# Nine feed-forward chunks instead of eleven carry modulation blocks, and the pooling stage eight instead of four

## The reference, cut to what matters

```
def trunk(x, c, ...):
    for i in range(2):
        shift1, scale1, gate1, shift2, scale2, gate2 = split(silu(c) @ w_ada[i] + b_ada[i], 6)
        h = rms_norm(x, g_mix[i]) * (1 + scale1) + shift1
        mix = attention(h) @ w_o            # layer 0: stick-breaking attention
        mix = pool_mixer(h, hist, w_pool)   # layer 1: trailing means over 2/4/8/16 frames, four 512x512 maps
        x = x + gate1 * mix
        h = rms_norm(x, g_ffn[i]) * (1 + scale2) + shift2
        x = x + gate2 * ((silu(h @ w_gate[i]) * (h @ w_up[i])) @ w_down[i])
```

## Time and profile before

| what | value |
|---|---|
| median of 3 runs | 3418.9 us (3418.2 to 3427.47) |
| the profiled execution | 3424.23 us |
| its span in the trace | 3422.4 us |
| TensorE busy | 3268.1 us, 95% of the span |
| VectorE busy | 2119.0 us, 62% |
| ScalarE busy | 1308.8 us, 38% |
| first feed-forward, about | 988 to 2182 us of the span |
| pooling stage with its norms, about | 2182 to 2317 us |
| second feed-forward, about | 2317 us to the end |

### The profile page before, as it was taken

How to read it: one execution, slowest core, us unless ns; L and a number is a source line. 1 busy time by engine, 2 the same in 40 slices (tenths; PEclk the granted TensorE clock), 3 DMA queues, 4 the chain that set the end, 5 groups by cost and what they waited for, 6 DMA issues and landing times.

```text
span 3422.4 us, 47948 instructions
## 1 busy us (share of the span) xinstructions
PE 3268.1 (95%) x20213; PEld 2952.9 (86%) x20213; DVE 2119.0 (62%) x1852; ACT 1308.8 (38%) x991; POOL 137.5 (4%) x124
## 2 busy tenths in 40 slices
PE   6999998889979999999999999769999999999999
PEld 3677776667979999999999999559999999999999
DVE  4488885557887767777776777784344443334443
ACT  3344444455453444344443443333322222332221
POOL 0000000000000000000000000100000000000000
PEclk9999999999989999999999999889999999999999
DMA  9777777877645555556555555544333333333341
GB/s 353 269 267 251 250 242 246 296 275 261 232 150 196 196 200 192 186 182 208 203 178 193 186 208 196 180 165 147 123 123 126 131 123 127 131 123 123 125 132 62
DMA packets 325816, 646.48 MB, mean 189 GB/s; under 512 B 10882, under 2 KB 13514, under 8 KB 325322
## 3 DMA queue, kind: packets, MB, share of 16 engines
q1 hardware_dynamic: 317144, 630.17, 54.1%
q10 hardware_dynamic: 8586, 15.09, 1.2%
HBM read 631.46 MB, written 14.74 MB: 189 GB/s over the span
## 4 chain that ended last, share of the span: by engine, by line
PE 87%; DVE 4%; DMA 4%; ACT 3%; issue 1%; ACTq 0%; POOL 0%; SPq 0%; DVEq 0%; POOLq 0%
PE bank L1495 24%; PE bank L1497 23%; PE bank L1496 23%; PE bank L1577 3%; PE bank L1522 3%; PE bank L1579 3%; PE bank L1578 3%; DMA raw<-in_w_ada 3%; PE bank L1683 1%; PE bank L1507 1%; DMA raw<-in_cache_k 1%; PE bank L1711 1%; PE bank L1712 1%; DVE w_lo L945 0%; PE bank L1531 0%
## 5 line engine op out<-in xcount | busy, mean ns | idle before, releaser
L945 DVE TENSOR_TENSOR w_lo<-raw,w_hi 128x2048 fp32r<-128x2048 f32 x323 | 738.9, 2290 | 877.7 <-ACT w_hi L568 877.7
L568 ACT ACTIVATE w_hi<-raw 128x2048 fp32r<-128x2048 f32 x323 | 616.3, 1915 | 1349.7 <-PE bank L1497 1169.4
L1495 PE MATMUL bank<-h_hi,w_hi 128*128 128x384 f32 x3136 | 1064.1, 339 | 33.0 <-DVE h_lo L1028 24.7
L1496 PE MATMUL bank<-h_lo,w_hi 128*128 128x384 f32 x3136 | 1052.1, 335 | 0.0
L1497 PE MATMUL bank<-h_hi,w_lo 128*128 128x384 f32 x3120 | 1047.8, 336 | 0.0
L1495 PEld LDWEIGHTS bank<-h_hi,w_hi 128*128 128x128 f32 x3136 | 591.8, 189 | 78.6 <-issue 69.1
L1496 PEld LDWEIGHTS bank<-h_lo,w_hi 128*128 128x128 f32 x3136 | 592.1, 189 | 0.0
L1497 PEld LDWEIGHTS bank<-h_hi,w_lo 128*128 128x128 f32 x3120 | 588.7, 189 | 0.0
L1495 PE MATMUL bank<-act_hi,w_hi 128*128 128x384 f32 x1408 | 473.1, 336 | 0.0
L1497 PE MATMUL bank<-act_hi,w_lo 128*128 128x384 f32 x1408 | 470.8, 334 | 0.0
L1496 PE MATMUL bank<-act_lo,w_hi 128*128 128x384 f32 x1408 | 470.7, 334 | 0.0
(11 more groups left out here) (225 smaller groups left out, 2506.1 us busy)
## 6 DMA issues: line engine op xcount, KB each, us to landing
raw<-in_w_ada SPq DMA_DIRECT2D x192, 1024.0 KB, 5.8
raw<-in_w_gate SPq DMA_DIRECT2D x88, 1024.0 KB, 5.2
raw<-in_w_up SPq DMA_DIRECT2D x88, 1024.0 KB, 5.2
raw<-in_w_down SPq DMA_DIRECT2D x88, 1024.0 KB, 5.1
raw<-in_w_qkv SPq DMA_DIRECT2D x40, 1024.0 KB, 5.3
raw<-in_cache_k SPq DMA_DIRECT2D x32, 1024.0 KB, 6.8
raw<-in_cache_v SPq DMA_DIRECT2D x32, 1024.0 KB, 7.7
raw<-in_w_o SPq DMA_DIRECT2D x15, 1024.0 KB, 5.1
```

Of the source, the lines that this page charges most:

```text
L568: act.activation(w_hi[:, s], raw[:, s], ACT.Copy).then_inc(hi_ready, 1)
L945: dve.tensor_tensor(w_lo[:, s], raw[:, s], w_hi[:, s].bitcast(f32), ALU.subtract).then_inc(lo_ready, 1)
L1495: pe.matmul(out, w, a, start=start, stop=False)
L1496: pe.matmul(out, w, al, start=False, stop=False)
```

## The change

The first feed-forward gets nine mixed chunks (`HOSTS`), eight in the loop and the ninth written out, and behind them two plain chunks, written out too, with the code of the second layer's chunks. So the last four blocks, the second layer's scale2, are no longer computed there. The pooling stage takes eight blocks: one before step 0, one at the end of each of the steps 0 to 6, behind the group's map where there is one. Every step has the transposes of a block. On ACT the copy to `mod` stands in every step, ahead of the two store DMAs instead of behind `h_hi`. SP loads eight blocks there, one after the other through the four slots, and the second feed-forward's first quarters behind them.

```diff
-W_POOL = W_FFN0 + 5 * CHUNKS
+HOSTS = 9
+W_PLAIN = W_FFN0 + 5 * HOSTS
+W_POOL = W_PLAIN + 3 * (CHUNKS - HOSTS)
-ADA_POOL = ADA_FFN + 2 * CHUNKS
+ADA_POOL = ADA_FFN + 2 * HOSTS
...
@@ SP
-            with sp.Fori(1, CHUNKS) as c:
+            with sp.Fori(1, HOSTS) as c:
                 load_mixed(W_FFN0 + c * 5, c, 1, c * 2 + (ADA_FFN - 24))
+            for c in range(HOSTS, CHUNKS):
+                W = W_PLAIN + 3 * (c - HOSTS)
+                load_cols(W, w_gate[0], c * 512)
+                load_cols(W + 1, w_up[0], c * 512)
+                load_down(W + 2, 0, c)
...
-            for i in range(3):
+            for i in range(7):
                 for s in range(4):
                     sp.wait_ge(ada_used, 4 * (ADA_QKV + i) + s + 1)
                     load_late(i + 1, s)
@@ ACT
-            def dense_chunk(W, c, last=False):
+            def dense_chunk(W, c, last=False, squares_after=False):
...
                 if not last:
-                    for n in range(12, 16):
-                        dense(W, n)
+                    for n in range(4):
+                        dense(W, 12 + n)
+                        if squares_after:
+                            square(2, n)
...
+                mod_out(4 * (ADA_QKV + j) + 4, ADA_POOL + j, 2, ada_used)
                 act.wait_ge(uT_taken, j + 1)
...
-                if j % 2 == 0:
-                    i = ADA_QKV + j // 2
-                    mod_out(4 * i + 4, ADA_POOL + j // 2, 2, ada_used)
@@ DVE
-            def dense_chunk(W, c, r, last=False):
+            def dense_chunk(W, c, r, last=False, sums_after=False):
...
                 for s in range(4):
-                    if not last:
+                    if not last and not (sums_after and s == 3):
                         dense(W, 12 + s)
-                    down_add(4 * W + 9 + s, s, r, 1)
+                    down_add(4 * W + 9 + s, s, r, 0 if isinstance(c, int) and c < CHUNKS else 1)
+                    if sums_after and s < 3:
+                        square_sum(2, s)
...
-            dense(W_FFN0 + 5 * (CHUNKS - 1), 23)
+            dense(W_POOL, 3)
...
-                if j % 2:
-                    mod_in(ADA_POOL + j // 2, 3, pieces=1)
+                mod_in(ADA_POOL + j, 3, pieces=1)
@@ PE
-            with pe.Fori(0, CHUNKS) as c:
+            with pe.Fori(0, HOSTS) as c:
                 mixed_chunk(W_FFN0 + c * 5, c, ADA_FFN + c * 2, R_FFN0 + c * 4, 4)
+            for c in range(HOSTS, CHUNKS):
+                dense_chunk(W_PLAIN + 3 * (c - HOSTS), c, R_FFN0 + c * 4, 4, half=1)
...
-                if j % 2:
-                    ada_turn(ADA_POOL + j // 2, 3)
-                elif j:
-                    ada_block(ADA_QKV + j // 2, 2)
+                ada_turn(ADA_POOL + j, 3)
                 if j >= 2 and j % 2 == 0:
                     map_group(j // 2 - 1)
+                if j < 7:
+                    ada_block(ADA_QKV + j + 1, 2)
```

More of the change, by code:

```diff
@@ L842, in gate_out, with mixed_chunk @@
                 act.activation(act_f[:], bank[:, 4:8, 0:TOK], ACT.Silu).then_inc(gate_taken, 1)
-            def mixed_chunk(W, c, a, following, last=False):
+            def mixed_chunk(W, c, a, following):
                 for n in range(4, 10):
@@ L858, in mixed_chunk @@
                     following(W, 20 + s)
-                    if last:
-                        square(2, s)
-            def dense_chunk(W, c, last=False):
+            def dense_chunk(W, c, last=False, squares_after=False):
                 for n in range(4, 7):
@@ L873, in dense_chunk @@
                 if not last:
-                    for n in range(12, 16):
-                        dense(W, n)
-            with act.Fori(0, CHUNKS - 1) as c:
+                    for n in range(4):
+                        dense(W, 12 + n)
+                        if squares_after:
+                            square(2, n)
+            with act.Fori(0, HOSTS - 1) as c:
                 mixed_chunk(W_FFN0 + c * 5, c, ADA_FFN + c * 2, mixed)
-            mixed_chunk(W_FFN0 + 5 * (CHUNKS - 1), CHUNKS - 1, ADA_FFN + 2 * (CHUNKS - 1), dense, last=True)
+            mixed_chunk(W_FFN0 + 5 * (HOSTS - 1), HOSTS - 1, ADA_FFN + 2 * (HOSTS - 1), dense)
+            for c in range(HOSTS, CHUNKS):
+                dense_chunk(W_PLAIN + 3 * (c - HOSTS), c, squares_after=c == CHUNKS - 1)
             root(2)
@@ L1368, in down_add, with mixed_chunk @@
                 add_quad(down_bank(s), 4 * s, layer, GATE2)
-            def mixed_chunk(W, c, a, layer, r, following, last=False):
+            def mixed_chunk(W, c, a, layer, r, following):
                 for n in range(4, 12):
@@ L1384, in mixed_chunk @@
                     down_add(4 * W + 17 + s, s, r, layer)
[L1385 to L1388, removed]
+                    following(W, 20 + s)
             def rows_out(q):
@@ L1402, in dense_chunk @@
                 for s in range(4):
-                    if not last:
+                    if not last and not (sums_after and s == 3):
                         dense(W, 12 + s)
-                    down_add(4 * W + 9 + s, s, r, 1)
+                    down_add(4 * W + 9 + s, s, r, 0 if isinstance(c, int) and c < CHUNKS else 1)
+                    if sums_after and s < 3:
+                        square_sum(2, s)
                     if last:
                         rows_out(s)
-            with loop(dve, 0, CHUNKS - 1, {step: 4 * ADD + 2}) as c:
+            with loop(dve, 0, HOSTS - 1, {step: 4 * ADD + 2}) as c:
                 mixed_chunk(W_FFN0 + c * 5, c, ADA_FFN + c * 2, 0, R_FFN0 + c * 4, mixed)
-            mixed_chunk(W_FFN0 + 5 * (CHUNKS - 1), CHUNKS - 1, ADA_FFN + 2 * (CHUNKS - 1), 0, R_FFN0 + 4 * (CHUNKS - 1), dense, last=True)
+            mixed_chunk(W_FFN0 + 5 * (HOSTS - 1), HOSTS - 1, ADA_FFN + 2 * (HOSTS - 1), 0, R_FFN0 + 4 * (HOSTS - 1), dense)
+            for c in range(HOSTS, CHUNKS):
+                dense_chunk(W_PLAIN + 3 * (c - HOSTS), c, R_FFN0 + 4 * c, sums_after=c == CHUNKS - 1)
             norm_coef(2)
@@ L1876, in turn_rows, with dense_chunk @@
                     last.then_inc(yT_done, 1)
-            def dense_chunk(W, c, r, hr, last=False):
+            def dense_chunk(W, c, r, hr, last=False, half=2):
                 pe.wait_ge(residual_taken, r - 1)
@@ L1884, in dense_chunk @@
                     else:
-                        pe.wait_ge(half_ready, 2)
+                        pe.wait_ge(half_ready, half)
                     to_features(W, j, 4, h_hi, h_lo, 4 * j, j == 0, j == 3, second_half=None if j else hr + 1)
```

## The result

The changed kernel takes 3440.1 us (median of 6 runs, 3438.3 to 3444.9) against 3421.3 us for the kernel before, timed beside it (6 runs, 3418.2 to 3427.5). The ratio is 1.006, interval 1.005 to 1.007, or +18.8 us. The forecast was +14.6 us, 3433.5 us, with a chance of 0.65 for slower. The profiled execution took 3438.3 us.

The account below looks back on a forecast made before the run. The prediction took TensorE as the bound, 87% of the chain, full in mixed chunks but partly idle in the pooling stage. -17.9 + 3.0 + 29.5 = +14.6 us on the median 3418.9 gave 3433.5 us, range 3414 to 3443.

Parts of the forecast that it names:

- The plain chunks and the split: First feed-forward: two chunks becoming plain remove 17.9 us; DVE's split ahead of the last addition adds 3.0 us.
- The sign named for it: End of the first feed-forward: last square 6 us behind the last down product instead of 3.
- The pooling stage: Four more blocks and turns and 16 MB of loads delay `pooled(3)` by 29.5 us, bounds +15.2 and +42.
- Steps 0 and 1: Pooling stage: loads at 2.7 us a quarter; second block done about 2213.5, step 1 ends at 2225 (2224 to 2226).
- Steps 3 and 5: Pooling steps without a map: wait for refilled slots, 12.2 us each, bounds 8.4 and 13.9.
- Step 2: Pooling step with a map: transposes, copies, turn, map and block in one string on TensorE, 17.0 us (15.1 to 19.7).
- Steps 4 and 6: Pooling steps with a map: the same string on TensorE, 17.0 us each, between 15.1 and 19.7.
- the last step: Step 7, from its transposes to `pooled(3)`: DVE's own work is the chain, 16.9 us, the last map covered.
- the pace of the loads: Pooling stage: queued quarter loads follow at 2.7 us each, 386 GB/s, so four slots reload in 10.9 us.
- The idle time: Rival, pooling stage: TensorE's waits absorb the blocks, stage grows by 1.7 us, total 3405.7 us; chance 0.10.
- The loads in time: Rival: quarters land as TensorE reaches them, steps 3 and 5 take 8.6 us, 7.2 less; total 3426.3; chance 0.16.
- A TensorE that stays cold through the maps: Rival, pooling stage: low clock persists, map 16.8 us, step with a map 26.0; total 3465 us; chance 0.08.

## Why the prediction was right

**The plain chunks and the split.** Both as forecast, -17.94 and +3.18 (forecast -17.9 and +3.0). The sign named for it, a last square 6 us behind its product, came as 6.24. Undoing the order alone gave the 3.18 back.

**The pooling stage.** The mechanism is the one forecast: blocks of steps 1, 3 and 5 in quarters with DMA as releaser, steps with a map without a break. The size was 3.0 us short, in parts that have both signs: steps 0, 1, 3 and 5 were 5.9 us longer than forecast, the three maps' steps and the last one 3.0 shorter. That the total came so near is in part luck. Steps 0 and 1 ended 2.7 later than forecast with the stage's start lined up: from the first block's last quarter to the second block's last it took 2195.01 - 2183.07 = 11.9 us, not four times 2.7, and step 1 took 12.7, not 11.5. Steps 3 and 5 took 14.4 and 13.2, forecast 12.2. The last quarter began 16.1 and 14.9 us behind the start of the block before (2236.93 - 2220.79, 2266.64 - 2251.71), forecast 15.1. It ran at the low clock (granted 0.50), 1.93 us instead of 1.5. And the block before ran in 3.64 us instead of 4.4, so that less of the refill lay beside it and more in the step that waits. Step 2 was 14.8, not 17.0: it took 2.6 up to its map, the map 2220.79 - 2212.26 = 8.5 and its block 3.6. Steps 4 and 6 (16.5 and 16.9) and the last step (16.7, forecast 16.9; its parts as listed add up to 17.1) came as worked out.

The step of the prediction that was too low is the pace of the loads: read from a single distance in the opening, which was among the shortest, with 0.7 us for the small transfers beside them in step 1 and nothing in step 0. The fourth quarter of step 3 came 2.72 us behind the third, 386 GB/s, but over the step's four it is (2236.93 - 2228.07) / 3 = 2.95 us, 355 GB/s, and in step 5 (2266.64 - 2258.32) / 3 = 2.77 us, 378 GB/s. The table of windows over these two stretches, and in each the DMA queue that carries the step's small transfers (packets, MB, share of the 16 engines):

```profile
2228.07:2236.93 8.86, 5.80 (x25) 0.62 (x25) 7.31 (x14) 0.83 (x3) 1.05 (x1) 0.50 1.04 373
2258.32:2266.64 8.32, 3.20 (x24) 0.48 (x24) 8.15 (x13) 1.50 (x4) 1.70 (x1) 0.92 1.06 395
```

```profile
q10 hardware_dynamic: 309, 0.27, 11.3%
q10 hardware_dynamic: 174, 0.15, 5.2%
```

The engines are full in both stretches; the small transfers took 11.3% of their time in the first and 5.2% in the second, and the loads had the rest. They took 8.2% in step 0 and 7.7% in step 1 up to the last quarter.

One page put the loads dearer (the Trainium skill, DMA: Bandwidth & Descriptors, section "Where 436 GB/s comes from", about 358 GB/s from HBM for one core). The sum by it, an estimate 2.5 us higher, would have come nearer to the measured time. These stretches do not show its limit, though: all queues together moved 373 and 395 GB/s.

**The rivals.** The idle time did not take the blocks: their quarters had not landed, as argued, and in the runs with shorter loads, where most of them had, it took nearly all of the added work. The loads in time had the right condition but too low a price, 7.2 us (by the terms shown 12.2 less 10.7 - 7.3 is 8.8 a step, so 6.8): it counted steps 3 and 5 alone, where the loads also held steps 0 and 1 and left the maps to start at a low clock. A TensorE that stays cold through the maps did not come. The prediction took a rule on how bursts start for one on how they go on. The map of step 2 had the full clock from its start, those of steps 4 and 6 began at the low one and ended at the full one: 8.5, 9.9 and 10.3 us instead of 16.8.

## What to carry to other kernels

An idle TensorE takes added work only if that work's operands can arrive in the idle time: before moving a block there, compare the time from the release of its buffer to the last landing with the time until the engine comes round again. Count buffers, not the DMA engines' mean share: eight blocks through four slots cost 32.5 us, and nearly the same traffic through more slots 2.2. Where a refill stands on the path, shortening the work beside it should gain nothing; no run here tested that.

## What I had not expected of the hardware

A block directly behind a map takes 3.64 us at a granted clock of 1.00, against 4.31 and 5.70 us at means of 0.83 and 0.63 in the kernel before; the prediction took the 4.3 for the full clock. A quarter that has waited took 1.93 us behind a wait of 0.79 us and 1.07 behind one of 1.93 us (2236.93 and 2263.93), so the length of the last wait alone does not tell its clock.
